# Router logits from x2, expert choice in two parts, block table by shift and scan, first gathers with direct indices

## The reference

```python
def hier_moe(xn, w_rg, b_rg, w_re, b_re, w1, w3, w2):      # xn = rmsnorm(x, ffn_norm_g)
    lg = einsum('td,dg->tg', xt, w_rg) + b_rg               # 4 groups
    pg_top, g_sel = top_k(softmax(lg), 1)
    le = einsum('td,gde->tge', xt, w_re) + b_re             # 8 experts in each group
    le = take_along_axis(le, g_sel[:, :, None], axis=1)[:, 0]
    pe_top, e_sel = top_k(softmax(le), 2)
    gate = pg_top * pe_top / sum(pe_top)
    ...
    # every token goes to its two experts; rows of one expert are put together in blocks
    h = silu(xb @ w1[e]) * (xb @ w3[e])
    out[token] += (h @ w2[e]) * gate
```

## Time and profile before

| | us |
|---|---|
| median of 3 runs | 1302.69 (1301.82 to 1305.11) |
| the profiled execution | 1302.61 |
| its span in the trace | 1300.9 |
| PE busy | 1131.4 (87%) |
| DVE busy | 520.4 (40%) |
| ACT busy | 424.4 (33%) |
| POOL busy | 261.6 (20%) |

### The profile page before, as it was taken

The page is one execution under the profiler, slowest core; times in us unless marked ns, Lnnn a source line. Parts: engine busy times, 40 slices in busy tenths (PEclk is TensorE's granted clock), DMA queues, the critical chain, the costliest instruction groups (busy, mean ns, idle before and its releaser), DMA issues.

```text
span 1300.9 us, 15822 instructions
## 1 busy us (share of the span) xinstructions
PE 1131.4 (87%) x5178; PEld 694.9 (53%) x5178; DVE 520.4 (40%) x890; ACT 424.4 (33%) x671; POOL 261.6 (20%) x279
## 2 busy tenths in 40 slices
PE   1999999999988977999983899989999879899940
PEld 1788888888856645888873333333333333333310
DVE  3551111112337756655445344343425334334217
ACT  4422222223146555433232133333324333324222
POOL 0010000000007001000000243424334224234302
PEclk9999999999989966999985999989999899899975
DMA  7153331711160002632288499999989999999325
GB/s 290 50 192 113 110 113 54 264 59 48 48 243 1 2 0 91 221 110 103 111 324 360 156 398 392 419 420 405 419 340 389 421 421 420 420 415 404 144 109 209
DMA packets 66591, 299.47 MB, mean 230 GB/s; under 512 B 8672, under 2 KB 8800, under 8 KB 41216
## 3 DMA queue, kind: packets, MB, share of 16 engines
q1 hardware_dynamic: 53488, 264.44, 51.3%
q0 software_dynamic: 13072, 34.63, 6.8%
HBM read 272.29 MB, written 35.91 MB: 237 GB/s over the span
## 4 chain that ended last, share of the span: by engine, by line
PE 62%; DMA 18%; DVE 8%; issue 6%; ACT 5%; SPq 1%; DVEq 1%; ACTq 0%; POOLq 0%; POOL 0%
DMA rawe<-in_w 16%; PE ps L824 12%; PE ps L541 12%; PE ps L542 12%; PE ps L543 12%; PE ps L845 4%; ACT cur L1148 2%; PE ps L640 1%; PE ps L661 1%; PE ps L814 1%; PE ps L673 1%; PE ps L758 1%; DVE x L1610 1%; DVE x L1608 1%; PE ps L652 1%
## 5 line engine op out<-in xcount | busy, mean ns | idle before, releaser
L824 PE MATMUL ps<-cur13a,xT 128*64 128x512 f32 x656 | 163.0, 641 | 37.2 <-DVEq L1590 36.4
L541 PE MATMUL ps<-whi,xTh 128*128 128x512 f32 x480 | 188.4, 392 | 6.4 <-DVE xTl L1238 4.3
L543 PE MATMUL ps<-whi,xTl 128*128 128x512 f32 x480 | 187.8, 391 | 0.0
L542 PE MATMUL ps<-wlo,xTh 128*128 128x512 f32 x480 | 187.7, 391 | 0.0
L845 PE MATMUL ps<-cur,hT 128*64 128x512 f32 x656 | 152.4, 607 | 4.3 <-ACTq L1151 4.3
L1182 DVE TENSOR_TENSOR wlo<-raw,whi 128x2048 fp32r<-128x2048 f32 x27 | 61.7, 2292 | 218.1 <-ACT whi L868 217.9
L824 PE MATMUL ps<-cur13b,xT 128*64 128x512 f32 x656 | 148.5, 592 | 0.0
L1566 DVE COPY xT<-ps 128x512 f32<-128x512 f32 x41 | 28.4, 692 | 295.8 <-PE ps L814 295.8
L824 PEld LDWEIGHTS ps<-cur13a,xT 128*64 128x64 f32 x656 | 52.9, 146 | 118.4 <-issue 116.1
L919 ACT ACTIVATE zst<-ps 128x512 f32<-128x512 f32 x60 | 35.9, 600 | 235.1 <-PE ps L543 235.1
L1148 ACT ACTIVATE cur<-rawe 128x4096 f32 x31 | 112.2, 3620 | 0.1
(11 more groups left out here) (219 smaller groups left out, 1483.0 us busy)
## 6 DMA issues: line engine op xcount, KB each, us to landing
rawe<-in_w SPq DMA_DIRECT2D x96, 2048.0 KB, 17.6
raw<-in_w_in SPq DMA_DIRECT2D x20, 1024.0 KB, 5.7
z_scratch<-zst POOLq DMA_DIRECT2D x60, 256.0 KB, 2.3
gat<-z_scratch SPq DMA_DIRECT2D x12, 512.0 KB, 3.7
xn_scratch<-rrow POOLq DMA_DIRECT2D x6, 1024.0 KB, 4.3
ya<-y_scratch SPq DMA_DIRECT2D x6, 1024.0 KB, 10.0
raw<-in_w_out SPq DMA_DIRECT2D x4, 1024.0 KB, 7.0
xin<-in_x_prompt SPq DMA_DIRECT2D x4, 512.0 KB, 8.6
```

The lines of the kernel that those rows point to most:

```text
L541: pe.matmul(out, ah, bh, start=first, stop=False)
L542: pe.matmul(out, ah, bl, start=False, stop=False)
L543: return pe.matmul(out, al, bh, start=False, stop=last)
L824: mm = pe.matmul(ps[0][u * CAP:(u + 1) * CAP, :], xT[:, c, h * CAP:(h + 1) * CAP], cur13[h][:, :, c * 512 + u * 256:c * 512 + u * 256 + 25 ...
```

## The change

1. wrt is multiplied once by the norm's weight (a column per partition, gcol, loaded by one more small DMA on SP; the product on POOL, signal s_wrg). PE transposes x2 itself instead of rrow, and the factor 1/rms of a token is applied when the bias is added (one instruction, as before).
2. `logits(t-1)` stands between the two parts of the second half of tile t, no longer at its end.
3. `rsqrt_column`, for one column, has 9 instructions in place of 12.
4. `choose` is called for tiles 0 to 3 before the last tile's additions, and for tiles 4 and 5 at the end; PE counts in two parts, the first of them ahead of logits(5).
5. Blocks of an expert come from an add, a shift and a max with multiply; their running sum is one scan. Both slots of a token come from one product and one sum over both tables.
6. Half of the one-hot pairs stand ahead of the bcol computation; PE's turn of bcol stands between the ninth and the tenth product.
7. Some waits of DVE on itself are gone around s_Ab, s_bc and s_nb. The first two gathers take their indices straight from idxt, and POOL reads nb behind the first gather.

Two tables of constants are gone, some tiles have other places.

```diff
@@ PE
             def route_columns(t):
-                pe.wait_ge(s_rr, t + 1)
+                pe.wait_ge(s_x2, 2 * t + 2)
...
-                        mm = pe.transpose(ps[j][:, c * P:(c + 1) * P], rrow[t % 2][:, 4 * j + c::KC], ident)
+                        mm = pe.transpose(ps[j][:, c * P:(c + 1) * P], x2[:, t, 4 * j + c::KC], ident)
...
             def logits(t):
                 pe.wait_ge(s_rTc, 2 * t + 2)
                 if t == 0:
-                    pe.wait_ge(s_rp, 16 * 3)
+                    pe.wait_ge(s_wrg, 1)
...
+                        if t >= 1 and n == 1 and j == 0:
+                            logits(t - 1)
                     mm.then_inc(s_w, 1)
                     if t >= 1 and n == 0:
                         route_columns(t - 1)
-                if t >= 1:
-                    logits(t - 1)
             route_columns(NT - 1)
+            def count(a, b, first, last):
+                pe.matmul(ps[3][:, a * NE:b * NE], C("tri"), picked[:, a * NE:b * NE],
+                          start=first, stop=False, skip_group_check=True)
+                for u in range(1, NT + 1 - a):
+                    w = min(b, NT + 1 - u)
+                    mm = pe.matmul(ps[3][:, (a + u) * NE:(w + u) * NE], C("ones"), picked[:, a * NE:w * NE],
+                                   start=False, stop=(last and u == NT - a), skip_group_check=True)
+                return mm
+            pe.wait_ge(s_Ab, 1)
+            count(0, NT - 2, True, False)
             logits(NT - 1)
-            pe.wait_ge(s_Ab, 1)
-            picked = Ab[:, :, :].rearrange("p t e -> p (t e)")
-            pe.matmul(ps[3][:, 0:NT * NE], C("tri"), picked, start=True, stop=False, skip_group_check=True)
-            for u in range(1, NT + 1):
-                mm = pe.matmul(ps[3][:, u * NE:(NT + 1) * NE], C("ones"), picked[:, 0:(NT + 1 - u) * NE],
-                               start=False, stop=(u == NT), skip_group_check=True)
-            mm.then_inc(s_rk, 1)
+            pe.wait_ge(s_Ab, 2)
+            count(NT - 2, NT, False, True).then_inc(s_rk, 1)
@@ DVE
+            def rsqrt_column(c, n_mean):
+                v, y, a, h = ssq[:, c:c + 1], rstd[:, c:c + 1], rs_a[:, c:c + 1], rs_a[:, 16 + c:17 + c]
+                dve.tensor_scalar(h, v, -0.5 / n_mean, -0.5 * EPS, ALU.mult, ALU.add)
+                link(dve.tensor_scalar(v, v, 1.0 / n_mean, EPS, ALU.mult, ALU.add))
+                link(dve.tensor_scalar(y.bitcast(I32), v.bitcast(I32), -0.5, float(0x5f3759df), ALU.mult, ALU.add))
+                for _ in range(3):
+                    link(dve.scalar_tensor_tensor(out=a, in0=y, scalar=y, in1=h, op0=ALU.mult, op1=ALU.mult))
                     link(dve.scalar_tensor_tensor(out=y, in0=a, scalar=1.5, in1=y, op0=ALU.add, op1=ALU.mult))
...
-                dve.tensor_tensor(lg[:, t, :], ps[2][:, 0:NG + NE], brt[:, :], ALU.add).then_inc(s_rx, 1)
+                dve.scalar_tensor_tensor(out=lg[:, t, :], in0=ps[2][:, 0:NG + NE], scalar=rstd[:, t:t + 1],
+                                         in1=brt[:, :], op0=ALU.mult, op1=ALU.add).then_inc(s_rx, 1)
...
+                if t + 1 < NT:
+                    merged_lo(t + 1)
+                else:
+                    choose(0, NT - 2)
...
-            choose(0, NT - 1)
             route_logits(NT - 1)
-            choose(NT - 1, NT)
+            choose(NT - 2, NT)
...
-            link(dve.tensor_tensor(over, cnt.unsqueeze(2).to_broadcast([P, NE, MAXB - 1]),
-                                   C("thr").unsqueeze(1).to_broadcast([P, NE, MAXB - 1]), ALU.is_gt))
-            link(dve.tensor_reduce(nov[:, :], over, AX.X, ALU.add))
-            Z0 = NE // 2
-            link(dve.tensor_copy(run[:, 0, Z0:], nov[:, :]))
-            a, d = 0, 1
-            while d < NE:
-                link(dve.tensor_tensor(run[:, 1 - a, Z0:], run[:, a, Z0:], run[:, a, Z0 - d:Z0 + NE - d], ALU.add))
-                a, d = 1 - a, 2 * d
...
+            link(dve.tensor_scalar(wint[:, :], cnt, float(CAP - 1), None, ALU.add))
+            link(dve.tensor_scalar(wint[:, :], wint[:, :], 6, None, ALU.logical_shift_right))
+            link(dve.tensor_scalar(wide[:, :], wint[:, :], 1.0, float(CAP), ALU.max, ALU.mult))
+            link(dve.tensor_tensor_scan(ends[:, :], wide[:, :], zero[:, :], 0.0, ALU.add, ALU.add))
+            link(dve.tensor_tensor(first[:, :], ends[:, :], wide[:, :], ALU.subtract))
...
-            for k, Ak in enumerate((A1, A2)):
-                link(dve.tensor_tensor(t2[:, :, :], t1[:, :, :], Ak[:, :, :], ALU.mult))
-                link(dve.tensor_reduce(slotf[:, k, :], t2[:, :, :], AX.X, ALU.add))
+            link(dve.tensor_tensor(t2[:, :, :, :], A12[:, :, :, :],
+                                   t1[:, :, :].unsqueeze(1).to_broadcast([P, 2, NT, NE]), ALU.mult))
+            link(dve.tensor_reduce(slotf[:, :, :], t2[:, :, :, :], AX.X, ALU.add))
...
-            link(dve.tensor_scalar(idxt[:, :], ps[4][:, 0:NB + 1], -2.0, C("half"), ALU.mult, ALU.add))
-            dve.sem_inc(s_nb, 1)
+            dve.tensor_scalar(idxt[:, :], ps[4][:, 0:NB + 1], -2.0, C("half"), ALU.mult, ALU.add).then_inc(s_nb, 1)
@@ POOL
+            pool.wait_ge(s_rp, 16 * 4)
+            pool.tensor_tensor(wrt[:, :, :], wrt[:, :, :], gcol[:, :].unsqueeze(2).to_broadcast([P, KC, NG + NE]),
+                               ALU.mult).then_inc(s_wrg, 1)
...
-            nb = pool.value_load(nbi[0:1, 0:1], min_val=NE, max_val=NB)
+            pool.sem_inc(s_idx, 1)
...
+                if isinstance(b, int) and b < 2:
+                    index = idxt[:, b:b + 1]
+                else:
+                    pool.tensor_copy(idxb[:, :], idxt[:, bass.ds(b, 1)]).then_inc(s_ic, 1)
+                    pool.wait_ge(s_ic, b - 1)
+                    pool.sem_inc(s_idx, 1)
+                    index = idxb[:, 0:1]
```

More of the change, by code:

```diff
@@ L804, in _ @@
                           start=(q == 0), stop=(q == 2 * NT - 1)).then_inc(s_tbm, 1)
+                if q == NT + 2:
+                    pe.wait_ge(s_bc, 1)
+                    pe.matmul(ps[5][0:1, 0:P], bcol[:, 0:1], ident, start=True, stop=True).then_inc(s_br, 1)
             pe.wait_ge(s_nb, 1)
@@ L1429, in _ @@
             merge_lo(7)
-            for t in range(NT):
-                if t + 1 < NT:
-                    merged_lo(t + 1)
-                dve.wait_ge(s_xr, 16 * (t + 1))
-                for n in range(2):
-                    dve.wait_ge(s_w, 2 * t + n + 1)
-                    dve.tensor_tensor(x2[:, t, n * 512:(n + 1) * 512], ps[6 + n][:, :],
-                                      xres[:, n * 512:(n + 1) * 512], ALU.add).then_inc(s_x2, 1)
-                dve.wait_ge(s_sq2, t + 1)
-                rsqrt(t, t + 1, D, link)
-                if t == 0:
-                    dve.wait_ge(s_rp, 16 * 3)
-                dve.scalar_tensor_tensor(out=rrow[t % 2][:, :], in0=x2[:, t, :], scalar=rstd[:, t:t + 1],
-                                         in1=g2[:, :], op0=ALU.mult, op1=ALU.mult).then_inc(s_rr, 1)
-                if t >= 1:
-                    route_logits(t - 1)
             def choose(a, b):
@@ L1506, in _ @@
-            while d < NE:
-                link(dve.tensor_tensor(run[:, 1 - a, Z0:], run[:, a, Z0:], run[:, a, Z0 - d:Z0 + NE - d], ALU.add))
-                a, d = 1 - a, 2 * d
-            incl = run[:, a, Z0:]
-            link(dve.tensor_tensor(first[:, :], incl, nov[:, :], ALU.subtract))
-            link(dve.scalar_tensor_tensor(out=first[:, :], in0=first[:, :], scalar=float(CAP), in1=C("ecap"),
-                                          op0=ALU.mult, op1=ALU.add))
+            link(dve.tensor_scalar(wint[:, :], cnt, float(CAP - 1), None, ALU.add))
@@ L1528, in _ @@
-            link(dve.scalar_tensor_tensor(out=last_row[:, :], in0=here.to_broadcast([P, NE]), scalar=float(CAP),
-                                          in1=first[:, :], op0=ALU.mult, op1=ALU.subtract))
-            link(dve.tensor_scalar(t2[:, 0, :], last_row[:, :], 0.0, None, ALU.is_ge))
-            link(dve.tensor_reduce(bcol[:, 2:3], t2[:, 0, :], AX.X, ALU.add))
-            link(dve.tensor_scalar(bcol[:, 0:1], bcol[:, 2:3], -1.0, None, ALU.add))
-            dve.sem_inc(s_bc, 1)
-            for q in range(2 * NT):
+            link(dve.tensor_copy(sbf[:, :, :, :], bp[:, :, :, :]))
@@ L1536, in _, with one_hot @@
+            def one_hot(q):
                 k, t = q // NT, q % NT
@@ L1542, in _ @@
                                   C("code")[:, q:q + 1], ALU.is_equal, ALU.mult).then_inc(s_tb, 1)
-            link(dve.tensor_scalar(nbi[:, 1:2], run[0:1, a, Z0 + NE - 1:Z0 + NE], float(NE - 1), None, ALU.add))
-            link(dve.tensor_scalar(nbi[:, 0:1], run[0:1, a, Z0 + NE - 1:Z0 + NE], float(NE), None, ALU.add))
+            for q in range(NT):
+                one_hot(q)
+            here = C("tok")[:, 0:1]
+            link(dve.scalar_tensor_tensor(out=last_row[:, :], in0=here.to_broadcast([P, NE]), scalar=float(CAP),
```

(13 more changed lines are left out.)

70 lines of the change are left out of this document (40 added, 30 removed).

## The result

| | before | changed |
|---|---|---|
| median of 7 runs, us | 1303.39 (1301.82 to 1305.11) | 1297.16 (1290.66 to 1298.48) |
| profiled execution, span | 1300.9 | 1296.4 |
| projection starts (ACT's first mTh) | 586.64 | 588.88 |
| gathered rows reach PE | 712.19 | 707.16 |
| from there to the end of the span | 588.7 | 589.2 |

The ratio of the times is 0.9946 with an interval of 0.9927 to 0.9964: 4.7 to 9.5 us faster. The medians differ by 6.2 us. The prediction was 1294.9 us, with a range of 1291.5 to 1299.5, so 7.7 to 7.8 us faster.

A forecast was written before the change was run, and what follows sets the result against it. It took a single file of waits from w_out's last product to the first gather's landing as the bound; summed step by step, landing moved from 712.14 to 704.5, so 1302.6 - 7.7 = 1294.9 us, range 1291.5 to 1299.5.

The forecast's parts named there:

- Output projection: Products of w_out on PE: moved logits(t-1) delay the last product, 1.7 us lost; choice of tiles 0 to 3 costs nothing.
- rival D: Within w_out: PE stalls at the moved logits(t-1) waiting for ACT's column copies; slower, 1306.9 us; chance 0.04.
- Logits of tile 5: Behind the last additions: logits(5) waits until DVE takes over tile 4's logits behind rrow, starting at 677.2.
- Clock: PE at logits(5): full clock because products cut up the pause, so it ends at 679.1.
- the other case: PE at logits(5): half clock, 1.8 us later, total 1296.8 us; chance 0.20.
- Choice, count, slots: From logits(5)'s take-over to the first one-hot: Ab at 683.85, ranks at 685.5, slots 3.4 us, first one-hot 688.9.
- One-hot tables: From first one-hot to idxt: 6.04 + 0.95 + 0.3 = 7.3 us, idxt at 696.2.
- Gather: POOL's first gather: issued 1.35 us after idxt instead of 2.44, landing in 6.9 us at 704.5.
- Rival B: First gather: it lands only when the weights' queue runs dry, at 712 again; 1302.6 us; chance 0.12.
- rival C: Experts' stage: the weight stream, not the first block, sets the end; gain given back, 1302.6 us; chance 0.04.
- The hole in the stream: DMA idle until expert 1's weights are copied out: some 16 us wide, shrinking to 8, so the stream starts earlier.
- Stretch: Output projection to the first gather's landing, all steps summed: 7.7 us gained, landing at 704.5 instead of 712.14.

The follow-up runs named there:

- e2: Changed kernel, but DVE takes over tile 4's logits ahead of the root and rrow of tile 5; median 1293.82 us, ratio to before 0.9942.
- e4: Changed kernel, but PE makes the first count behind logits(5) instead of ahead of it; 1298.54 us in one run.
- e1: Changed kernel with logits(t-1) put back to the end of tile t; median 1296.49 us, ratio to before 0.9943.
- e6: Changed kernel, but POOL reads nb ahead of the first gather and every gather uses the copied index column; 1296.03 us in one run.
- e3: Changed kernel, but SP issues expert 2's weights only when the first gather has landed; median 1293.15 us, ratio to before 0.9924.
- e7: Changed kernel, but POOL clears xg behind s_rr, ahead of its wait for the stores' landing; 1297.22 us in one run.
- e8: Changed kernel with the edits of e1, e2, e3, e4 and e7 together; median 1289.82 us, ratio to before 0.9895.
- e5: Changed kernel with the old choice (tiles 0 to 4, then 5, behind the last rrow) and one count of all six; 1303.64 us in one run.

## Why the prediction was right

**Output projection.** Predicted 1.7 us lost, measured 1.9 (last product 85.34 instead of 83.44 us into the projection; 0.13 of the other 0.2 is that the twelve products behind the moved logits start over 2.62 us instead of 2.49). The choice of tiles 0 to 3 was hidden, as said, but with less room: it ended at 671.6, 82.7 us into the projection and not 80.9, and DVE then waited 2.4 us for PE's last half where the prediction had 4. PE never waits for ACT or DVE within w_out, so rival D is out.

**Logits of tile 5.** The step on which most hung, that logits(5) doesn't follow the early transposes but waits until DVE frees the bank behind rrow, was right and e2 confirmed it. Start predicted 90.6 us into the projection, measured 91.05. The 0.5 are the 0.2 above and an instruction price that the prediction had wrong: `scalar_tensor_tensor` with a column as scalar takes 0.22 us where the old root's instructions took 0.16, three in the root, and 0.25 instead of 0.19 for taking over logits.

**Clock.** Full clock, as forecast; logits(5) 1.95 us (1.9). e4 gave the other case 1.6 us on the stretch (1.8), and bears out the reason given, the products between the pauses. e1 shows how narrow it was: behind a pause of 1.18 the clock fell within logits(5), and about a third of the price was paid.

**Choice, count, slots.** From the take-over to the end of Ab 4.8 us (4.7), from there to the ranks 1.6 (1.6), slots 3.42 (3.4); the scan, with no row to go by, was 0.23, near the end of its range that was taken.

**One-hot tables.** Predicted 7.3, measured 7.53; the 0.2 are the clearing of xg, which the prediction had given 5 us of room for its own end without asking what it would run beside.

**Gather.** 1.22 us from idxt (1.35; the two terms that the prediction names, 0.28 and 0.81, make 1.09, so the rest of its 1.35 had no row). Landing 6.64 (6.9). Rival B is out twice: it landed with 8 us of the stream still to come, and e6's landing moved with its issue.

**The rest.** The tail is 589.2 against 588.7, so nothing was given back that the scatter of the tail (587.7 to 591.4) doesn't hold; rival C is out. The hole in the stream took up the difference, as said, but the prediction had its size wrong: it said 16 us, shrinking to 8. It was about 20 and shrank to about 10: measured from the start of the projection, the weights of expert 3 start 7 us sooner, and the stream ahead of them ends 2 us later.

Stretch: predicted 7.7, measured 7.3. The steps hold one by one, but that the sum is off by only 0.4 is in part luck: logits, choice and one-hot tables came 0.8 us late in all, count, gather and landing some 0.4 early. Median: 6.2, interval 4.7 to 9.5. The 1 us between stretch and medians isn't a step of the sum; it is within what start and tail scatter.

**What no experiment isolates.** Two parts of the change are only read from the traces. With the transposes on x2, logits(5) starts 1.59 us behind the start of rrow where it started 4.00 behind it: 2.4 us nearer. The block table by shift and scan takes 3.42 us from ranks to first one-hot in place of 6.53, but the one-hot tables, which now hold the bcol work, take 7.53 in place of 6.04: 1.6 us net.

## What to carry to other kernels

Where several engines hand work on in a single file, follow the bank or buffer that the next step needs, not only its data: here the early operand brought logits(5) 2.4 us nearer to rrow (read from the traces), and the wait for the bank kept back another 2.0, which one moved line gave (e2). Work that is put into a pause of TensorE can pay by the clock alone, and work moved ahead of the last product of a stage is paid in full by all that follows it. Prefetches aren't free while a small transfer is on the path: hold the one that isn't needed yet (3.7 us here, e3).

## What the runs showed of the hardware

- A gather of 128 half rows (256 KB) took 2.94 us from issue to use with the DMA engines nearly idle, 3.63 beside the rest of one stream, and 6.6 to 6.9 beside a full one. The Trainium skill ("DMA: Bandwidth & Descriptors", "SWDGE vs HWDGE vs iDMA") has the engines go round-robin between the two kinds of queue; the traces agree that the gather gets through, but at more than double the time.
- POOL's clearing of 128x512 held up a DVE instruction of 0.28 us to 0.69. The Trainium skill ("SBUF — State Buffer", "SBUF: two separate sides") says that POOL and DVE share a pair of ports as an exclusive lock, which one of them holds for a whole instruction, and that on DVE's side only some kinds of instructions take it. Six traces agree, and e7, where the clearing ran elsewhere, does too. So do two traces in which it ran beside other kinds: in e4, at 688.82, beside a sum over 384 elements (TENSOR_REDUCE) that took its usual 0.55 us, and in e8, at 676.33, beside small instructions of the choice at their usual 0.16 and 0.17. Only TENSOR_SCALAR was held.
- The scatter from run to run isn't spread over the kernel: the stretch repeats to 0.1 us, while the tail goes with the clock of PE in the first block. The first 16 records of it on PE's timeline in e4:

```profile
707.46 6.65 PE L835 MATMUL ps<-cur13a,xT 128*64 128x512 f32 x16 [0.78 <-DVE xT L1578]
```

And in the first trace of the changed kernel:

```profile
709.07 5.79 PE L835 MATMUL ps<-cur13a,xT 128*64 128x512 f32 x16 [0.78 <-DVE xT L1578]
```

With 6.65 and 6.64 (e5) the tails are 591.4 and 591.3, with 5.79 and 5.86 (e8) they are 589.2 and 589.3, and with 5.00 (e2) 587.7. The other traces lie between in the same order, within 0.2 us. The mean granted clock in the 6 us from the first record on is 0.50 in e4 and e5, 0.64 in the changed kernel and 0.77 in e2. No experiment set this clock, so it is a correlation. Why a late clock costs more than the first block's own difference is open.
